# Modulation's rows one step ahead, latents' units early, compression units one by one, in a two-block kernel on one core

## The chip, the cores and the metric

The kernel runs on one core of one Trainium2 chip. The metric is the device time of one execution in microseconds (us). A core has five engines that run their own queues in order and meet at semaphores: TensorE (PE, matrix products into eight PSUM banks of 128 x 512 floats), VectorE (DVE), ScalarE (ACT), GpSimd (POOL) and SyncE (SP, which here only issues transfers). Behind SP's issues 16 DMA engines move the data from HBM.

## The reference, cut to what matters

Two transformer blocks over one sequence of 256 tokens, width 1024, in float32. What the change touches is the front of the first block:

```python
mod = (silu(c) @ w_ada + b_ada)                      # 6 x 1024: shift, scale, gate for attention and FFN
h = rms_norm(x, attn_norm) * (1.0 + scale_a) + shift_a
(nq, nkc, nvc, nks, nvs, nkw, nvw, ngate, cq, ckv, kr, bgate) = split(h @ w_in)
q_a = rope(rms_norm(heads(nq, 8), nsa_q_norm), pos)
kc = rms_norm(compress(rope(heads(nkc, 2), pos), cmp_k_pe, cmp_k_w1, cmp_k_w2), nsa_kc_norm)
vc = compress(heads(nvc, 2), cmp_v_pe, cmp_v_w1, cmp_v_w2)      # silu(blocks @ w1) @ w2
ks, kw = rope(rms_norm(nks)), rope(rms_norm(nkw))
q_b = rms_norm(cq, mla_cq_norm) @ w_uq               # latent cq: 384 wide
kv_b = rms_norm(ckv, mla_ckv_norm) @ w_ukv           # latent ckv: 256 wide; kr: rope part of the keys
```

Behind it come sparse and latent attention, the output projection, a gated FFN with a short convolution, and the second block; the change leaves their code as it is. All weights together are some 200 MB, each read once.

## The kernel before, in words

**Units.** Every weight matrix is cut into units of at most 1 MB. `_order()` (L62) writes down by hand in which order they are loaded; SP loads unit i into raw buffer i mod 5 (`sp_program`, L2451) and first waits until unit i-5 is used up (`freed`, L2438). SP's queue is in order, so a late buffer holds back every load behind it. A product is made of three float32r products of high and low parts: ACT copies the raw unit to a high part in two halves (`split_hi`, L330), DVE subtracts for the low part (`split_lo`, L340), PE multiplies (L386, L404). There are two buffers of each, so the high part of a unit waits until PE is done with the unit two before. `next_hi` and `next_lo` convert the unit behind the named one. Three kinds of units (ada, ck1, cv1) are used raw.

**Modulation.** Units ada 0 to 7 give scale and shift of the attention norm in four rounds. In round j PE multiplies ada 4+j and ada j into one row bank (`ada_rows_pe`, L504), ACT copies the bank to `rows[j % 2]` (L521), PE turns four pieces of it into columns of the same bank (`ada_turn_pe`, L528), DVE adds the bias and multiplies the two chunks 2j and 2j+1 of x with gain and rstd (`tail_dve`, L657), ACT and DVE split them into `H` (`tail_act`, L637). The rows of round j+1 wait until DVE has read the columns. Later units ada 8 to 10 are summed on DVE (`ada_dve`, L541), added over partitions by PE into a bank of ring G (`ada_sums_pe`, L563) and read by `mod_dve`.

**First projections.** wa (kc, vc, q0, q1: 48 matmuls) and wb (q2, q3: 24 matmuls) are cut along the contraction: pair j needs only chunks 2j and 2j+1 of `H`. `head_pe` (L620) runs statistics of x, rows 0, turn 0 and then, for each j: wa j, rows j+1, turn j+1, wb j.

**Banks.** PSUM banks 0 to 2 are ring G, 3 to 6 ring M (`Ring.take(reader)`, L127: the next bank in turn, and who must have read it before). Bank 7 holds the norm's statistics and the compression networks' sums. SBUF rings of four squares (`four_ring`), two rstd buffers and four temporaries work in the same way; a taker waits for the reader of its predecessor in the buffer.

**The other projections.** `proj_pe` (L872) and its ACT and DVE twins run win 0 (ks), 1 (kw), 4, 5, 6 (cq, ckv, kr), between them the rope and norm products of kc, q0 to q3 (`head_pe2`, L712), and behind each of win 4, 5, 6 two units of a compression network (`cmp2_pe`, 16 matmuls a unit, L772). `latent_pe` (L956) then runs win 2 and 3 (values), cv 2 and 3, the networks' second layers (`hidden_*`, `key_*`, `value_*`), the latents' statistics in bank 7 (`stat_pe`), ada 8, the gate rows wg, the rope of kr, uq 0 to 2, ada 9, ukv 0 and 1 with the MLA norms (`mla_stat_pe`), ada 10. The MLA tables are made on POOL (`latent_pool`, L1199) once the value product is copied.

Of the kernel before, what the change touches and what calls it, by code (L numbers as in the profile page):

```python
# [144 lines left out]
def build(nc, ins, out):  # L145
# [496 lines left out]
    def head_act(act):  # L642
# [8 lines left out]
        for j in range(4):  # L651
            ada_rows_act(act, j)
            tail_act(act, j)
            split_hi(act, ("wa", j))
            split_hi(act, ("wb", j))
# [2034 lines left out]
```

## Time and profile before

| | us |
|---|---|
| median of 3 runs (lowest, highest) | 1211.31 (1210.5, 1212.99) |
| the profiled execution's own time | 1205.75 |
| its span, first to last instruction | 1204.4 |
| PE busy in the span | 1134.9 (94%) |
| DVE busy | 749.7 (62%) |
| ACT busy | 591.0 (49%) |
| mean granted clock of TensorE | 0.972 |

The profiled execution is a run of its own, with its own time; sums over its rows stand against 1205.75, not against the median. Granted clock 1.00 is 2.4 GHz, 0.50 is 1.2 GHz. Times in rows are us from the start of the span; L386 is line 386 of the kernel. A row that begins with an engine and ends with an arrow names who ended the wait.

### The profile page before, as it was taken

What the parts mean: (1) busy time and instruction counts of PE and PEld (TensorE: products, weight loads), DVE (VectorE), ACT (ScalarE), POOL (GpSimd) and SP (SyncE); (2) the same over time, 40 slices, a digit from 0 to 9 for tenths busy, and PEclk for the clock granted to TensorE, in tenths of its full rate; (3) what the DMA queues carried; (4) which work ended last, traced back from release to release, by engine and by line L of the source; (5) the groups of instructions that cost most, each with busy time, mean ns of one, the idle gap of its engine ahead of it and who ended that gap; (6) DMA issues with size and microseconds to landing.
All of it is one profiled execution on the core that took longest, in us unless ns stands there. A gap on an engine that the chain in (4) does not pass through costs nothing.

```text
span 1204.4 us, 19238 instructions
## 1 busy us (share of the span) xinstructions
PE 1134.9 (94%) x7774; PEld 1027.3 (85%) x7774; DVE 749.7 (62%) x1411; ACT 591.0 (49%) x1046; POOL 27.8 (2%) x32
## 2 busy tenths in 40 slices
PE   5899789999999999999999899999999989999998
PEld 4797479888878999888988689999878968999986
DVE  2454567688757878866556666665455556666644
ACT  3362547345547566534434565445456357544533
POOL 0050100000000000001000000000000000000000
PEclk8999889889989999999989899999999999999999
DMA  8776362344334555465543265554544414655450
GB/s 323 300 288 248 122 236 106 105 175 175 141 105 158 175 180 189 143 259 211 190 143 105 70 234 206 175 181 175 176 168 158 140 42 138 223 177 185 147 192 35
DMA packets 30797, 207.81 MB, mean 173 GB/s; under 512 B 3540, under 2 KB 4052, under 8 KB 7157
## 3 DMA queue, kind: packets, MB, share of 16 engines
q1 hardware_dynamic: 30708, 206.58, 48.3%
q8 instruction: 62, 1.02, 0.3%
q14 instruction: 27, 0.21, 0.1%
HBM read 205.52 MB, written 1.05 MB: 172 GB/s over the span
## 4 chain that ended last, share of the span: by engine, by line
PE 84%; DVE 8%; ACT 5%; issue 2%; DMA 1%; SPq 0%; ACTq 0%; DVEq 0%
PE ps L386 47%; PE ps L1563 18%; PE ps L614 2%; DVE wlo L345 2%; PE ps L404 2%; ACT whi L338 1%; PE ps L2164 1%; PE ps L2196 1%; DVE tm L557 1%; PE ps L1262 1%; DMA raw<-win 1%; PE ps L1688 1%; PE ps L1340 1%; PE ps L516 1%; PE ps L772 1%
## 5 line engine op out<-in xcount | busy, mean ns | idle before, releaser
L345 DVE TENSOR_TENSOR wlo<-raw,whi 128x1024 fp32r<-128x1024 f32 (+2 forms) x328 | 370.9, 1174 | 246.1 <-ACT whi L338 246.0
L386 PE MATMUL ps<-H_h,whi 128*128 128x256 f32 x1552 | 447.0, 288 | 2.5 <-DVE wlo L345 2.5
L386 PE MATMUL ps<-H_l,whi 128*128 128x256 f32 x1552 | 440.9, 284 | 0.0
L386 PE MATMUL ps<-H_h,wlo 128*128 128x256 f32 x1552 | 440.8, 284 | 0.0
L338 ACT ACTIVATE whi<-raw 128x1024 fp32r<-128x1024 f32 (+2 forms) x328 | 314.8, 1010 | 183.6 <-PE ps L1563 112.9
L386 PEld LDWEIGHTS ps<-H_h,whi 128*128 128x128 f32 x1552 | 300.1, 193 | 6.9 <-issue 6.6
L386 PEld LDWEIGHTS ps<-H_l,whi 128*128 128x128 f32 x1552 | 299.9, 193 | 0.7 <-issue 0.5
L386 PEld LDWEIGHTS ps<-H_h,wlo 128*128 128x128 f32 x1552 | 299.5, 193 | 0.0
L1563 PE MATMUL ps<-whi,gl_h 128*128 128x512 f32 x264 | 105.6, 400 | 0.5 <-DVE wlo L345 0.5
L1563 PE MATMUL ps<-whi,gl_l 128*128 128x512 f32 x264 | 104.7, 396 | 0.0
L1563 PE MATMUL ps<-wlo,gl_h 128*128 128x512 f32 x264 | 104.6, 396 | 0.0
L1786 ACT ACTIVATE uw<-uw 128x256 f32<-128x256 f32 x66 | 27.4, 415 | 86.5 <-DVE uw L1877 86.4
L1563 PEld LDWEIGHTS ps<-whi,gl_h 128*128 128x128 f32 x264 | 49.7, 188 | 13.4 <-DVE wlo L345 1.4
L1563 PEld LDWEIGHTS ps<-wlo,gl_h 128*128 128x128 f32 x264 | 49.7, 188 | 12.1
L1563 PEld LDWEIGHTS ps<-whi,gl_l 128*128 128x128 f32 x264 | 49.7, 188 | 11.6
L1825 DVE SCALAR_TENSOR_TENSOR uw<-ps,par_sb,uw 128x255 f32<-128x255 f32 (+1 forms) x88 | 36.4, 476 | 25.2 <-ACT uw L1774 25.2
L1774 ACT ACTIVATE uw<-ps,par_sb 128x256 f32<-128x256 f32 x44 | 22.5, 562 | 46.5 <-PE ps L386 46.5
L557 DVE SCALAR_TENSOR_TENSOR tm<-raw,cs,tm 128x256 f32<-128x256 f32 x96 | 40.7, 479 | 0.0
L614 PE MATMUL ps<-H_h,whi 128*128 128x256 f32 x96 | 28.5, 297 | 8.3 <-DVE wlo L345 8.3
L1877 DVE TENSOR_TENSOR uw<-ps,rn 128x512 f32<-128x512 f32 x44 | 30.1, 684 | 2.3 <-PE ps L386 2.0
L1796 ACT ACTIVATE gl_h<-tm 128x256 fp32r<-128x256 f32 x66 | 27.5, 417 | 2.7 <-DVE tm L1792 2.7
L1563 PE MATMUL ps<-whi,H_h 128*128 128x512 f32 x64 | 26.2, 410 | 2.3 <-DVE wlo L345 2.0
(440 smaller groups left out, 1526.4 us busy)
## 6 DMA issues: line engine op xcount, KB each, us to landing
raw<-f SPq DMA_DIRECT2D x44, 1024.0 KB, 4.9
raw<-win SPq DMA_DIRECT2D x27, 1024.0 KB, 5.7
raw<-ada SPq DMA_DIRECT2D x24, 1024.0 KB, 5.9
raw<-up SPq DMA_DIRECT2D x22, 1024.0 KB, 4.9
raw<-g SPq DMA_DIRECT2D x20, 1024.0 KB, 4.8
raw<-pw SPq DMA_DIRECT2D x12, 1024.0 KB, 4.9
raw<-down SPq DMA_DIRECT2D x10, 1024.0 KB, 5.1
raw<-wa SPq DMA_DIRECT2D x4, 1024.0 KB, 7.5
```

Of the source, the lines that this page charges most:

```text
L338: act.activation(whi[j % NS][:, a:b], raw_of(key)[:, a:b], ACT.Copy).then_inc(w_hi.hit(key, half), 1)
L345: dve.tensor_tensor(wlo[j % NS][:, a:b], raw_of(key)[:, a:b], whi[j % NS][:, a:b].bitcast(F32), ALU.subtract).then_inc(w_lo.hit(key, half), 1)
L386: ins_ = pe.matmul(bank[:, m * 256:(m + 1) * 256], wt[a][:, kt * w + col + m * 128:kt * w + col + m * 128 + 128], act[b][:, k0 + kt, :], s ...
L404: ins_ = pe.matmul(bank[:, t * width:(t + 1) * width], act[b][:, kt, t * 128:(t + 1) * 128], wt[a][:, kt * w + col:kt * w + col + width], ...
L557: dve.scalar_tensor_tensor(out=o, in0=w, scalar=cs[:, kt:kt + 1], in1=o, op0=ALU.mult, op1=ALU.add).then_inc(ada_sum.hit(u, kt), 1)
L614: ins_ = pe.matmul(where["win", name][:, m * 256:(m + 1) * 256], wt[a][:, c:c + 128], H[b][:, k, :], start=k == 0 and m == 0 and i == 0, s ...
L1563: ins_ = pe.matmul(b[t][:], act[h][:, k0 + kt, t * 128:(t + 1) * 128], wt[a][:, kt * 512:(kt + 1) * 512], start=k0 + kt == 0 and i == 0 an ...
L1774: act.activation(w[:, m, :], z[:, m, :], ACT.Identity, bias=pc("b_conv", 2 * c + m), scale=pc("w_conv", (2 * c + m) * 3 + 2)).then_inc(u_i ...
L1786: act.activation(w[:, g, :], w[:, g, :], ACT.Silu).then_inc(u_silu.hit(n, c), 1)
L1796: act.activation(gl[0][:, c, :], where["tm", n, c][:, 0:256], ACT.Copy).then_inc(g_hi.hit(n, c), 1)
L1825: dve.scalar_tensor_tensor(out=w[:, m, s:], in0=z[:, m, 0:256 - s], scalar=pc("w_conv", (2 * c + m) * 3 + 2 - s), in1=w[:, m, s:], op0=ALU ...
L1877: dve.tensor_tensor(uw[c % 3][:], v2(where[n, c][:]), bc2(rn[:]), ALU.mult).then_inc(u_rn.hit(n, c), 1)
```

## The change

- Load order: the ada units come earlier against wa and wb; win 4, 5, 6 come before win 1, 2, 3; ck1 and cv1 units are spread one behind each win or uq unit; wg before ada 8.
- Rows: `ada_rows_pe(j)` waits for ACT's copy of row j-1 (`ada_row`) instead of DVE's reading; the turned columns go to bank 7, columns 256 + 4j. PE's order in the head is written out, as are ACT's and DVE's. 14 matmuls of ones with ones are put ahead of the statistics.
- `proj_*`: order win 0, 4, 5, 6, 1, 2, 3; the latents' squares are taken with the copy into their own buffers (`ckq`, two of them the modulation's row buffers), their statistics go to ring M (`latent_stat_pe`), their norms are done here; ck 0 to 3 and cv 0 one unit behind each. ACT's conversion of the unit after next ahead of the ks copy goes.
- `latent_*`: wg, rope of kr, key product, cv 1, uq 0, key norm, ada 8, cv 2, uq 1, cv 3, uq 2, hidden layer of v, ada 9, ukv 0 with the value product in its middle. POOL's MLA tables no longer wait for the value copy.
- Four buffers move: `xb` to the place of `X`, `hid` behind `ckvn`, `krb` to `rn`, `sqkr` into a row buffer; x^T is therefore loaded before ada 11, when cv 3 is done.

The diff below leaves out the ACT and DVE twins where they follow PE's order, and code that moves as a block.

```diff
@@ -66,11 +66,14 @@
     def seq(name, a=0, b=None):
         out.extend((name, i) for i in range(a, len(UNITS[name]) if b is None else b))
 
-    for i in range(4):
-        seq("ada", 4 + i, 5 + i), seq("ada", i, i + 1), seq("wa", i, i + 1), seq("wb", i, i + 1)
-    seq("win", 0, 2), seq("win", 4, 5), seq("ck1", 0, 2), seq("win", 5, 6), seq("ck1", 2, 4), seq("win", 6, 7)
-    seq("cv1", 0, 2), seq("win", 2, 3), seq("cv1", 2, 4), seq("win", 3, 4), seq("ada", 8, 9)
-    seq("wg"), seq("uq", 0, 2), seq("ada", 9, 10), seq("uq", 2), seq("ukv", 0, 1), seq("ada", 10, 11), seq("ukv", 1)
+    seq("ada", 4, 5), seq("ada", 0, 1), seq("wa", 0, 1), seq("ada", 5, 6), seq("ada", 1, 2), seq("wb", 0, 1)
+    seq("wa", 1, 2), seq("ada", 6, 7), seq("ada", 2, 3), seq("ada", 7, 8), seq("ada", 3, 4), seq("wb", 1, 2)
+    for i in (2, 3):
+        seq("wa", i, i + 1), seq("wb", i, i + 1)
+    seq("win", 0, 1), seq("win", 4, 6), seq("ck1", 0, 1), seq("win", 6, 7), seq("ck1", 1, 2), seq("win", 1, 2)
+    seq("ck1", 2, 3), seq("win", 2, 3), seq("ck1", 3, 4), seq("win", 3, 4), seq("cv1", 0, 1), seq("wg"), seq("ada", 8, 9)
+    seq("cv1", 1, 2), seq("uq", 0, 1), seq("cv1", 2, 3), seq("uq", 1, 2), seq("cv1", 3, 4), seq("ada", 9, 10), seq("uq", 2)
+    seq("ukv", 0, 1), seq("ada", 10, 11), seq("ukv", 1)
     seq("win", 7, 10), seq("ada", 11, 13), seq("win", 10, 11), seq("ada", 13, 14), seq("win", 11, 12)
     seq("ada", 14, 16), seq("win", 12, 13), seq("ada", 16, 17), seq("win", 13, 14), seq("ada", 17, 19)
     seq("win", 14, 15), seq("ada", 19, 20), seq("wo")
...
+    ckq = [sb("ckq", [128, 512]), rows[1], rows[0]]
     xc = [sb(f"xc{i}", [128, 2, 256]) for i in range(2)]
     hrow = [sb(f"hrow{i}", [128, 256]) for i in range(2)]
+    cw2 = [sb(f"cw2{i}", [128, 256]) for i in range(2)]
+    place[0] = X_at
     xb = [sb(f"xb{i}", [128, 32, 32]) for i in range(2)]
     place[0] = attn
     grow = sb("grow", [24, 256])
...
@@ -509,7 +515,7 @@
             if u == 4:
                 pe.wait_ge(*c_silu(2))
             elif c0 == 0:
-                pe.wait_ge(*mod_set(j - 1))
+                pe.wait_ge(*ada_row(j - 1))
             r = raw_of(("ada", u))
             for kt in range(8):
                 g = 32 * (kt % 4)
@@ -525,13 +531,15 @@
             act.wait_ge(*ada_col(j - 2))
         act.activation(rows[j % 2][:], where["rows"][:], ACT.Copy).then_inc(ada_row.hit(j), 1)
 
+    def mod_cols(j):
+        return banks[7][:, 256 + 4 * j:260 + 4 * j]
+
     def ada_turn_pe(pe, j):
 
-        b = where["rows"]
         pe.wait_ge(*ada_row(j))
         pe.wait_ge(*const_set("pick"))
         for m in range(4):
-            ins_ = pe.matmul(b[:, m:m + 1], rows[j % 2][:, m * 128:m * 128 + 128], pick[:, 0:1], start=True, stop=True)
+            ins_ = pe.matmul(mod_cols(j)[:, m:m + 1], rows[j % 2][:, m * 128:m * 128 + 128], pick[:, 0:1], start=True, stop=True)
         ins_.then_inc(ada_col.hit(j), 1)
 
     def asum(u):
...
@@ -619,19 +627,28 @@
 
     def head_pe(pe):
         pe.wait_ge(*const_set("ones"))
-        where["rows"], _ = M.take(mod_set(3))
+        where["rows"], _ = M.take(ada_row(3))
         for name in FIRST:
             ring = G if name in FIRST[0:3] else M
             where["win", name], _ = ring.take(z_copy(name) if name in ("kc", "vc") else z_sq(name))
+        for _ in range(14):
+            pe.matmul(where["rows"][:, 0:128], ones[:], ones[:], start=True, stop=True)
         for p in range(4):
             stat_pe(pe, "x0", p, where["sq", "x0", p], 2, p == 0, p == 3, sq_set("x0", p))
         ada_rows_pe(pe, 0)
         ada_turn_pe(pe, 0)
-        for j in range(4):
+        first_pe(pe, "wa", 0)
+        ada_rows_pe(pe, 1)
+        first_pe(pe, "wb", 0)
+        ada_turn_pe(pe, 1)
+        ada_rows_pe(pe, 2)
+        first_pe(pe, "wa", 1)
+        ada_turn_pe(pe, 2)
+        ada_rows_pe(pe, 3)
+        first_pe(pe, "wb", 1)
+        ada_turn_pe(pe, 3)
+        for j in (2, 3):
             first_pe(pe, "wa", j)
-            if j < 3:
-                ada_rows_pe(pe, j + 1)
-                ada_turn_pe(pe, j + 1)
             first_pe(pe, "wb", j)
...
+    def latent_stat_pe(pe, n, k0, m):
+
+        sm, old = M.take(rs_ln(n))
+        if old:
+            pe.wait_ge(*old)
+        where["sm", n] = sm
+        for k in range(k0, k0 + m):
+            pe.wait_ge(*sq_set("ck", k // 2))
+            ins_ = pe.matmul(sm[:, 0:256], ones[:], ckq[k // 2][:, k % 2 * 256:k % 2 * 256 + 256], start=k == k0,
+                             stop=k == k0 + m - 1)
+        ins_.then_inc(ones_done.hit(n), 1)
...
     def proj_pe(pe):
         gemm_pe(pe, ("win", 0), H, held, z_sq("ks"))
         pe.wait_ge(*con_in())
         head_pe2(pe, "kc")
+        gemm_pe(pe, ("win", 4), H, held, sq_set("ck", 0))
+        head_pe2(pe, "q0")
+        gemm_pe(pe, ("win", 5), H, held, sq_set("ck", 1))
+        head_pe2(pe, "q1")
+        cmp_pe(pe, "ck", 0)
+        gemm_pe(pe, ("win", 6), H, held, sq_set("ck", 2))
+        latent_stat_pe(pe, "vs", 0, 3)
+        head_pe2(pe, "q2")
+        cmp_pe(pe, "ck", 1)
         gemm_pe(pe, ("win", 1), H, held, z_sq("kw"))
-        head_pe2(pe, "q0")
-        for i in range(3):
-            gemm_pe(pe, ("win", 4 + i), H, held, ev_act("ck", i))
-            head_pe2(pe, ("q1", "q2", "q3")[i])
-            if i == 2:
-                hidden_pe(pe, 0)
-            cmp2_pe(pe, *(("ck", 0), ("ck", 2), ("cv", 0))[i])
+        latent_stat_pe(pe, "vw", 3, 2)
+        head_pe2(pe, "q3")
+        cmp_pe(pe, "ck", 2)
+        values_pe(pe, "vs", ("win", 2))
+        head_pe2(pe, "ks")
+        cmp_pe(pe, "ck", 3)
+        values_pe(pe, "vw", ("win", 3))
+        head_pe2(pe, "kw")
+        hidden_pe(pe, 0)
+        cmp_pe(pe, "cv", 0)
...
         next_hi(act, ("win", 0))
         first("q2")
         first("q3")
-        next_hi(act, ("win", 1))
         head_copy_act(act, "ks", where["win", 0], unit("win", 0))
         next_hi(act, ("win", 4))
+        latent_copy_act(act, 0)
         head_act2(act, "q0")
+        next_hi(act, ("win", 5))
+        latent_copy_act(act, 1)
+        head_act2(act, "q1")
+        next_hi(act, ("win", 6))
+        latent_copy_act(act, 2)
+        latent_rstd_act(act, "vs", 3)
+        for k in range(3):
+            norm_hi(act, "vs", k, cqn)
+        head_act2(act, "q2")
+        next_hi(act, ("win", 1))
         head_copy_act(act, "kw", where["win", 1], unit("win", 1))
...
@@ -982,6 +1068,8 @@
             pe.wait_ge(*old)
         where["pm", "kr"] = pm
         pe.matmul(pm[:, 0:256], cc("perm32"), CK[:, 5, :], start=True, stop=True).then_inc(perm_done.hit("kr"), 1)
+        key_pe(pe)
+        cmp_pe(pe, "cv", 1)
         for i in range(3):
             for half in range(2):
                 b, old = G.take(ev_act("uq", i, half))
@@ -998,6 +1086,11 @@
                 pe.wait_ge(*gt_set(1))
                 pe.transpose(b[:, 0:24], grow[:, 0:128], cc("ident")[0:24, 0:24])
                 pe.transpose(b[:, 24:48], grow[:, 128:256], cc("ident")[0:24, 0:24]).then_inc(gt_turn.hit(), 1)
+                key_norm_pe(pe)
+                ada_sums_pe(pe, 8)
+            if i < 2:
+                cmp_pe(pe, "cv", 2 + i)
+        hidden_pe(pe, 1)
         ada_sums_pe(pe, 9)
         for half in range(4):
             b, old = G.take(ev_act("ukv", 0, half))
@@ -1006,6 +1099,8 @@
             where["ukv", 0, half] = b
             mm_fm(pe, ("ukv", 0), ckvn, normed("vw") if half == 0 else held, b, half * 256,
                   done=unit.hit("ukv", 0) if half == 3 else half_done.hit("ukv", 0, half))
+            if half == 1:
+                value_pe(pe)
             pm, old = M.take(rope_b("mq", half))
...
@@ -1089,6 +1168,7 @@
                 dst = mq[:, c0:c0 + 2, :] if i < 2 else mqr[:, c0 - 8:c0 - 6, :]
                 act.activation(dst, v2(where["uq", i, half][:]), ACT.Copy).then_inc(ev_act.hit("uq", i, half), 1)
         next_hi(act, ("ukv", 0))
+        hidden_act(act, 1)
         for half in range(4):
...
@@ -1145,14 +1207,20 @@
             next_lo(dve, ("uq", i))
             if i == 0:
                 ada_dve(dve, 9)
+            if i == 1:
+                key_norm_dve(dve)
+                mod_dve(dve, 8)
         dve.wait_ge(*gt_turn())
         dve.tensor_copy(gt[:], where["gt"][:, 0:48].rearrange("p (t g) -> p t g", g=24)).then_inc(gt_set.hit(2), 1)
         mod_dve(dve, 9)
         next_lo(dve, ("ukv", 0))
+        hidden_dve(dve, 1)
         for half in range(4):
             mq_rope_dve(dve, half)
             if half:
                 mq_norm_dve(dve, half - 1)
+            if half == 2:
+                value_dve(dve)
         next_lo(dve, ("ukv", 1))
         ada_dve(dve, 10)
         for half in range(4):
@@ -1197,7 +1265,6 @@
             m_rope.hit("mk", p), 1)
 
     def latent_pool(pool):
-        pool.wait_ge(*cmp_set("v"))
         table_pool(pool, "mq", "mq_rope", "mq_rsw", "cosr", "sinr")
...
                 sp.dma_start(con[:], ins["con"]).then_inc(con_in.hit(), 16)
-            if key == ("win", 4):
+            if key == ("ck1", 0):
                 load_bc(sp, 0)
-                sp.wait_ge(*n_lo("A", 7))
+            if key == ("win", 1):
                 for k, n in enumerate(("ck2", "cv2")):
                     sp.dma_start(cw2[k][:], ins[n].rearrange("(p f) -> p f", p=128)).then_inc(cw2_in.hit(k), 16)
             if key in BC_AT:
                 n, last = BC_AT[key]
                 sp.wait_ge(*mt_mul(last, 1, 1))
                 load_bc(sp, n)
-            if key == ("win", 6):
+            if key == ("ada", 11):
+                sp.wait_ge(*unit("cv1", 3))
                 sp.dma_start(X[:].rearrange("p t d -> p (t d)"), ins["xt"]).then_inc(xt_in.hit(), 16)
```

## Rows read from the trace of the kernel before

**Rows 1.** The page, part 1: busy us (share) and instructions of each engine.

```profile
PE 1134.9 (94%) x7774; PEld 1027.3 (85%) x7774; DVE 749.7 (62%) x1411; ACT 591.0 (49%) x1046; POOL 27.8 (2%) x32
```

**Rows 2.** Stretches: us; busy us of PE, PEld, DVE, ACT, POOL; clock, DMA share, GB/s.

```profile
20.40:72.70 52.30, 46.07 (x410) 42.07 (x411) 21.48 (x39) 18.08 (x29) 9.76 (x10) 0.97 0.79 299
72.70:175.40 102.70, 88.50 (x664) 73.27 (x663) 57.34 (x91) 44.19 (x79) 12.01 (x12) 0.92 0.55 204
175.40:205.00 29.60, 28.81 (x179) 26.44 (x177) 23.11 (x46) 23.88 (x41) 0.00 (x0) 1.00 0.35 139
```

**Rows 3.** Stretches, short ones, same columns.

```profile
0.00:10.00 10.00, 2.74 (x7) 2.24 (x8) 1.00 (x12) 3.68 (x6) 0.20 (x4) 1.00 0.83 317
20.30:23.70 3.40, 3.24 (x15) 3.24 (x16) 2.44 (x4) 0.84 (x2) 0.00 (x0) 0.50 0.70 266
126.20:133.00 6.80, 6.00 (x39) 2.61 (x38) 4.33 (x9) 1.70 (x4) 0.00 (x0) 0.50 0.11 28
...
154.80:160.30 5.50, 5.50 (x22) 5.13 (x23) 0.42 (x1) 0.00 (x0) 0.00 (x0) 0.50 0.85 311
```

**Rows 4.** PE's waits, 12.3 to 72.7 us: sum, times, longest.

```profile
PE ps L614 <- DVE wlo L345: 8.3, 4, 4.4
PE ps L534 <- ACT arow L526: 3.1, 4, 0.8
```

**Rows 5.** The chain of waits in time, 26 to 43 us: start, us, what.

```profile
27.90 1.91 PE ps L516 x32
...
30.54 1.07 PE ps L534 x8
```

**Rows 6.** PE's waits, 72.7 to 175.4 us.

```profile
PE ps L573 <- DVE tm L557: 8.1, 1, 8.1
...
PE ps L726 <- DVE tm L738: 2.1, 1, 2.1
PE ps L788 <- DVE tm L738: 1.1, 1, 1.1
```

**Rows 7.** Timeline of PE, the start: start, us, instruction, count, idle before.

```profile
7.26 3.35 PE L455 MATMUL ps<-sq,ones 128*128 128x256 f32 x8 [7.26 <-ACT sq L447]
10.45 1.89 PE L455 MATMUL ps<-zt,ones 128*128 128x256 f32 x8
```

**Rows 8.** DMA issues of 95.2 to 97 us: count, KB each, median us to landing.

```profile
raw<-cv SPq DMA_DIRECT2D x2, 1024.0 KB, 7.5
raw<-win SPq DMA_DIRECT2D x1, 1024.0 KB, 4.7
```

**Rows 9.** Timelines of ACT, DVE and POOL between 79 and 93 us.

```profile
86.78 0.60 ACT L710 ACTIVATE sq<-ps 128x512 f32<-128x512 f32 x1 [5.77 <-PE ps L726]
...
79.61 2.36 DVE L345 TENSOR_TENSOR wlo<-raw,whi 128x1024 fp32r<-128x1024 f32 x2 [2.44 <-ACT whi L338]
...
88.36 3.12 DVE L345 TENSOR_TENSOR wlo<-raw,whi 128x1024 fp32r<-128x1024 f32 x2 [4.46 <-ACT whi L338]
...
83.98 6.42 POOL L936 TENSOR_TENSOR xb<-xc,par_sb 128x240 f32<-128x240 f32 x8 [14.30 <-DVE xc L741]
```

**Rows 10.** The chain of waits in time, between 84 and 147 us.

```profile
86.75 5.74 PE ps L386 x48
...
94.21 1.86 PE ps L772 x32
...
145.73 0.99 PE ps L851 x8
```

**Rows 11.** Timeline of DVE, 164 to 170 us.

```profile
164.75 1.82 DVE L345 TENSOR_TENSOR wlo<-raw,whi 128x1024 fp32r<-128x1024 f32 x2
166.49 0.61 DVE L554 TENSOR_SCALAR tm<-raw,cs 128x256 f32<-128x256 f32 x2
167.01 2.46 DVE L557 SCALAR_TENSOR_TENSOR tm<-raw,cs,tm 128x256 f32<-128x256 f32 x6
```

**Rows 12.** The chain of waits in time, 175 to 179 us.

```profile
175.85 1.80 ACT whi L338 x2
```

More of the change, by code:

```diff
@@ L209, in build @@
     ckvn = pair("ckvn", 2)
+    hid = [sb(f"hid{i}", [128, 2, 30]) for i in range(4)]
     place[0] = mv_at
@@ L650, in head_act @@
         rstd(act, "x0", stat("x0", 3), D, banks[7][:, 0:256], rst[0])
[L651 to L655, printed above, removed]
+        ada_rows_act(act, 0)
+        tail_act(act, 0)
+        split_hi(act, ("wa", 0))
+        split_hi(act, ("wb", 0))
+        ada_rows_act(act, 1)
+        split_hi(act, ("wa", 1))
+        tail_act(act, 1)
+        ada_rows_act(act, 2)
+        split_hi(act, ("wb", 1))
+        tail_act(act, 2)
+        ada_rows_act(act, 3)
+        split_hi(act, ("wa", 2))
+        tail_act(act, 3)
+        for key in (("wb", 2), ("wa", 3), ("wb", 3)):
+            split_hi(act, key)
     def tail_dve(dve, j):
-        b = where["rows"]
+        b = mod_cols(j)
         dve.wait_ge(*ada_col(j))
@@ L866, in gemm_pe, with latent_rstd_act, latent_norm_dve, values_pe @@
         mm_fm(pe, key, act, ready, b, 0, by_k=by_k, done=unit.hit(*key), hook=hook)
-    def cmp2_pe(pe, nm, a):
-        cmp_pe(pe, nm, a)
-        cmp_pe(pe, nm, a + 1)
+    def latent_stat_pe(pe, n, k0, m):
[8 more added lines that the diff above has]
+        ins_.then_inc(ones_done.hit(n), 1)
+    def latent_rstd_act(act, n, m):
+        buf, old = rst_ring.take(n_mul(n, m - 1))
+        where["r", n] = buf
+        rstd(act, n, ones_done(n), 128 * m, where["sm", n][:, 0:256], buf, free=old)
+    def latent_norm_dve(dve, n, k0, m, lat, gain):
+        dve.wait_ge(*rs(n))
+        for k in range(m):
+            x = temp(dve, ("tm", n, k), n_lo(n, k))
+            dve.scalar_tensor_tensor(out=x[:, 0:256], in0=CK[:, k0 + k, :], scalar=pc(gain, k),
+                                     in1=where["r", n][:, 0:256], op0=ALU.mult, op1=ALU.mult).then_inc(n_mul.hit(n, k), 1)
+            if k:
+                norm_lo(dve, n, k - 1, lat)
+        norm_lo(dve, n, m - 1, lat)
+    def values_pe(pe, n, key):
+        b, old = G.take(ev_act(n))
+        if old:
+            pe.wait_ge(*old)
+        where[key] = b
+        mm_tm(pe, key, H, held, b, 0, 256, unit.hit(*key))
     def proj_pe(pe):
@@ L887, in latent_copy_act, with values_act @@
         act.activation(CK[:, 2 * i:2 * i + 2, :], v2(where["win", 4 + i][:]), ACT.Copy).then_inc(ev_act.hit("ck", i), 1)
+        act.activation(ckq[i][:], where["win", 4 + i][:], ACT.Square).then_inc(sq_set.hit("ck", i), 1)
+    def values_act(act, n, key, dst):
+        act.wait_ge(*unit(*key))
+        act.activation(dst[:], v2(where[key][:]), ACT.Copy).then_inc(ev_act.hit(n), 1)
     def proj_act(act):
@@ L916, in proj_dve @@
         next_lo(dve, ("win", 0))
-        next_lo(dve, ("win", 1))
         head_dve2(dve, "kc")
@@ L956, in latent_pe @@
     def latent_pe(pe):
-        for n, key, k0, m in (("vs", ("win", 2), 0, 3), ("vw", ("win", 3), 3, 2)):
-            b, old = G.take(ev_act(n))
-            if old:
-                pe.wait_ge(*old)
-            where[key] = b
-            mm_tm(pe, key, H, held, b, 0, 256, unit.hit(*key))
-            if n == "vs":
-                head_pe2(pe, "ks")
-                key_pe(pe)
-                cmp2_pe(pe, "cv", 2)
-                head_pe2(pe, "kw")
-            else:
-                hidden_pe(pe, 1)
-                key_norm_pe(pe)
-            for k in range(m):
-                stat_pe(pe, n, k, where["sq", n, k], 1, k == 0, k == m - 1, sq_set(n, k))
-        value_pe(pe)
-        ada_sums_pe(pe, 8)
         b, old = G.take(gt_exp())
@@ L1058, in latent_act @@
     def latent_act(act):
-        for n, key, dst, lat, k0, m in (("vs", ("win", 2), vs, cqn, 0, 3), ("vw", ("win", 3), vw, ckvn, 3, 2)):
-            if n == "vw":
-                next_hi(act, key)
-            act.wait_ge(*unit(*key))
-            act.activation(dst[:], v2(where[key][:]), ACT.Copy).then_inc(ev_act.hit(n), 1)
-            if n == "vs":
-                head_act2(act, "ks")
-                key_act(act)
-                cmp_row_act(act, 1)
-            else:
-                head_act2(act, "kw")
-                hidden_act(act, 1)
-                key_norm_act(act)
-            for k in range(m):
-                square(act, CK[:, k0 + k, :], n, k, ev_act("ck", (k0 + k) // 2), n=256, ring=four_ring)
-            buf, old = rst_ring.take(n_mul(n, m - 1))
-            where["r", n] = buf
-            rstd(act, n, stat(n, m - 1), 128 * m, banks[7][:, 0:256], buf, free=old)
-            for k in range(m):
-                norm_hi(act, n, k, lat)
-        sq_ring.free[:], zt_ring.free[:] = four_ring.free[0:2], four_ring.free[2:4]
         next_hi(act, ("wg", 0))
```

79 lines of the change are left out of this document (43 added, 36 removed).

## The prediction

> **What bounds the kernel now.** I read the page's engine totals first, then the stretches of the span, then the waits and the chain inside the stretches that the change touches. TensorE (PE) is busy for 94% of the span [rows 1], so only PE's own idle or slow time can be won. The table of stretches says where that is [rows 2]: from 20.4 to 72.7 us (the first projections) PE is busy 46.07 of 52.30 us, from 72.7 to 175.4 (the other projections, compression networks, latents) 88.50 of 102.70, from 175.4 to 205.0 28.81 of 29.60. The 999.4 us behind 205.0 run code that the change leaves as it is. At stake are 6.2 + 14.2 us idle, and what PE loses where its clock was granted at 0.50 (1.2 instead of 2.4 GHz), which is half of its busy time there: 3.24 / 2 = 1.6 us in the first stretch and (6.00 + 5.50) / 2 = 5.75 us in the second [rows 3].
>
> The first stretch's idle is 3 rounds of about 0.77 + 1.27 us: of the four waits of each kind in the view the first lies before it, at the start [rows 4]. PE computes a round of modulation rows (1.91), waits for ScalarE's copy, turns them (1.07) [rows 5], projects with the old half of the weights and waits for DVE's low part of the next. The second stretch's idle is one wait of 8.1 us before the sums of modulation unit 8 and four smaller ones, 2.1 and 1.1 among them, that make the other 6 [rows 6].
>
> The profiled execution took 1205.75 us, 1.35 more than its span. The median of the runs is 1211.31, 5.56 higher. I sum against the former and carry the difference over to the latter.
>
> **A, the start: -0.9 us.** 14 matmuls of ones are put before the statistics. PE idles there until the squares come at 7.26. Of the 8 statistic matmuls the first four take 3.35 us and the last four 1.89 [rows 7], so PE was at 1.2 GHz for the first four. Fourteen of half that width cost 14 x 0.42 = 5.9 us at 1.2 GHz (3.35 / 4 / 2 each), from 1.1 to 7.0: hidden, and PE comes warm to 7.26. The statistics then end at about 10.7 instead of 12.3. Modulation units 4 and 0 must have landed: 317 GB/s over the first 10 us [rows 3] is 3.17 of the 3.35 MB of parameters, x and both units, so they are there at about 10.5. All that follows is 1.65 earlier. The stretch at 1.2 GHz up to 23.7 stays, I assume; it held 15 matmuls in 3.24 us and now holds 23, and each of these 8 is worth 0.12 at the end: 0.9 is what arrives. Bounds: 0 (no warming) to -2.5 (the slow stretch goes too).
>
> **B, rows one step ahead: -5.9 us.** The rows of round j+1 wait only for the copy of round j, since the turned columns go to bank 7. wb(0) lies between rows 1 and their turn, so the copy lies under 2.9 us of matmuls. Round by round: rows 1 from 27.0, wb(0) from 28.9, turn 31.8, rows 2 from 32.9 to 34.8; wa(1) needs normalised chunk 2, made from the turn's end by DVE, ScalarE and DVE in 2.2 us: 35.1. That is the one wait, 0.3. Afterwards each low part is ready before its turn. SP's queue: modulation unit 2 is issued when PE has used unit 5 (28.0) and lands 4.7 us later [rows 8] at 32.7, 1 us before PE asks. 6.2 - 0.3 = 5.9. Bounds: -6.2, and -3 if each transfer lands as late as the 7.5 us of a queued one [rows 8]. The head ends at 72.7 - 6.8 = 65.9.
>
> **C, units behind units: -6.7 us.** The old losses go: 14.2 idle + 5.75 slow = 19.95. Two new waits come.
> First: ScalarE's queue has the square of ks before the high part of win 5. It overwrites the buffer that q0's ones-matmul reads and so waits for that matmul: 5.77 us in the old kernel [rows 9]. There PE had a whole unit (5.74) [rows 10] in between; now win 5 is the very next unit behind q0. Square 0.6, first high half 1.0, first low half 1.2, with their handovers 2.9 us: PE waits that. The POOL tables for MLA, moved up from behind the value sums to right behind the windows, lie beside this conversion. A low part beside POOL's windows took 3.12 for two halves, 2.36 alone [rows 9]; half of 0.76 is 0.4. Together 3.3. Bounds 2.5 to 4.5.
> The Trainium skill (SBUF — State Buffer, on the port pair of DVE and GpSimd) says that an operation of DVE with two SBUF inputs and a GpSimd operation that reads SBUF exclude each other for a whole instruction. The 3.12 beside the 2.36 agrees in kind; by the rule in full the first half could stand behind one whole POOL instruction, 0.8 by the windows' row (6.42 for 8), and the wait would be 3.7.
> Second, the large one: the sums of modulation 8 take the third G bank. Counting takes of that ring of three (win 0, 4, 5, 6, 1, 2, 3, gate weights, key, uq 0 twice), it is the bank of the key product, free once DVE has made the normalised key. On DVE that step stands behind the low part of uq 2, and this behind all the sums of modulation 9. Behind the waiting PE instruction are queued compression unit cv 2, all of uq 1 and of uq 2. The race runs from K, the end of kw's ones-matmul. DVE: rstd on ScalarE 1.35, last rope product 0.65, hidden layer 1.0, low part of uq 0 1.8, sums of modulation 8 0.6 + 2.5 [rows 11]: K + 7.9, which frees its raw buffer. Only then SP issues cv 3, modulation 9 and uq 2, in this order. The first of three lands after 4.7, the second 2.5 later [rows 8]: K + 15.1. Sums of 9 3.1, low part of uq 2 1.8 [rows 11], key 0.3: K + 20.3. PE: hidden layer 0.6, two compression units 2 x 0.93, gate rows 24 x 0.12 = 2.9, rope of kr 0.4, key 0.5, uq 0 36 x 0.12 = 4.3, turns 0.35 [rows 10]: K + 10.9. PE waits 9.4 us. In the old kernel PE was at 1.2 GHz for 5.5 us after its 8.1 us of waiting [rows 3, 6]; I take the same, a loss of 2.7. Together 12.0. Bounds 0 to 15.
> The work that leaves the stretch (value product 0.99 [rows 10], second hidden layer 0.63, sums of modulation 9 0.43) is 2.05. The stretch becomes 102.7 - 19.95 - 2.05 + 3.3 + 12.0 = 96.0.
>
> **D, the 29.6 us behind it: +1.2.** The value product, 0.99, now lies in a stretch that PE fills. The second hidden layer and the sums of 9 lie under ScalarE's conversion of ukv 1 (1.80) and the square behind it [rows 12], which stays; the exponential adds 0.2 to it. DVE's 1.0 for the hidden layer and 0.4 for the copy go into its idle time. Bounds 0.8 to 2.5.
>
> **At nothing:** x^T is loaded behind win 9 instead of beside win 6, where SP's queue is idle, and its reader comes some 100 us later. cw2's wait for the norm goes; nobody waited for it. kr's square is saved (0.4 of a ScalarE that waits anyway). Behind 205.0, E = 0, bounds -2 to +3 for slow stretches that fall otherwise.
>
> Sum: -0.9 - 5.9 - 6.7 + 1.2 = -12.3. Own time 1205.75 - 12.3 = 1193.45; as a median 1211.31 - 12.3 = 1199.0.
>
> **Rivals.**
> 1. The clock falls at the first new wait too: 3.3 us before win 5 send PE to 1.2 GHz, as from 126.2 on, behind waits of 2.1 and 1.1 [rows 3, 6]. A stretch of 6.8 us like that one, less what of it is idle, costs 3.0: -9.3, 1202.0. Against: two waits in each round before 63 us (0.8 and 1.3) did not cool it.
> 2. The ring wait isn't there or is hidden, since I count takes: 12.0 more is gained, 1187.0. Against: the count and the order on DVE are plain to read.
> 3. The reordering doesn't do what it says: each old wait of the second stretch is replaced by one of like length, because SP's chain of five buffers, each freed by the step before it, sets the pace. C = 0: -5.6, 1205.7. For: two new waits worth 15.3 against 19.95 are already in my sum. Against: in my walk the other transfers have 5 us to spare.
> 4. Slower: behind the long wait before modulation 8's sums PE stays at 1.2 GHz. Each us there costs 0.5, so 2 x (12.3 + 2.4) = 29 us more at 1.2 GHz, to about 185, make it +2.4: 1213.7. From there on it decides. For: the wait is longer than the old one. Against: after 8.1 us of waiting PE was back within 5.5 us [rows 3].
>
> **Chances.** Forecast 0.52 (own range 1195 to 1203), rival 1 0.17, rival 2 0.12, rival 3 0.11, rival 4 0.05, no change 0.03. The range of 1190 to 1206 holds the forecast, rival 1, rival 3 and the side of rival 2 on which only a part of the wait goes; what it leaves out is the rest of rival 2, rival 4 and no change. A measurement of this kernel can't tell less than 0.2% (2.4 us) from no change. Faster is all but rival 4 and no change: 0.92, same 0.03, slower 0.05.
>
> **What would show it.** A: 8 statistic matmuls in about 3.5 us. B: PE's waits for ScalarE's copy gone, the head's last matmul near 65.9. C: ScalarE's square of ks waiting some 8 us, and PE then some 3 for DVE's low part; PE idle some 9 us before modulation 8's sums with DVE's key step as releaser, at about 137 to 147. D: last matmul before the attention near 192.7. Wrong: no idle before those sums (rival 2), a head that ends behind 69, or PE at 1.2 GHz for more than 20 of the first 200 us.

## The result, and the profile after

The changed kernel takes 1194.69 us (median of 4 runs, 1193.6 to 1199.0) beside 1211.07 for the kernel before; the ratio is 0.9869, 95% interval 0.9842 to 0.9896. That is 16.4 us less, where 12.3 were forecast (1199.0, range 1190 to 1206). Five further rounds (e1) gave 1197.05 beside 1211.28, ratio 0.9894 (0.9862 to 0.9926). The forecast's own narrower range, 1195 to 1203, is missed by 0.3 in the first and holds the second. The two first profiled executions are only 6.75 apart (1199.0 and 1205.75), and the forecast for the changed kernel's own, 1193.45, is missed by 5.6; why is told below.

The page of the changed kernel, part 1, and its stretches (columns as in [rows 2]; the ends lie where the head, uq 2 and ukv 1 end, the answers to [rows 2]):

```profile
PE 1139.8 (95%) x7802; PEld 1033.5 (86%) x7802; DVE 748.5 (62%) x1411; ACT 590.9 (49%) x1043; POOL 25.9 (2%) x32
```

```profile
20.40:64.90 44.50, 44.02 (x404) 41.04 (x404) 20.15 (x37) 18.04 (x29) 9.31 (x10) 0.96 0.85 340
64.90:165.90 101.00, 86.41 (x655) 71.73 (x653) 55.13 (x87) 43.86 (x75) 10.61 (x12) 0.92 0.50 186
165.90:196.80 30.90, 30.45 (x190) 27.62 (x189) 24.18 (x50) 24.00 (x42) 0.00 (x0) 1.00 0.53 214
81.90:85.30 3.40, 3.33 (x15) 3.36 (x16) 3.33 (x5) 3.37 (x6) 1.76 (x1) 0.50 0.31 82
...
150.80:157.00 6.20, 6.17 (x31) 4.08 (x31) 0.42 (x1) 0.00 (x0) 0.00 (x0) 0.50 0.13 36
```

The head ends at 64.9 instead of 72.7, its idle of 6.2 us [rows 2] is 0.5. The middle stretch is 101.0 long instead of 102.7: 14.6 us idle, and two slow stretches, 81.9 to 85.3 and (0.50 from 143.4 on) 150.8 to 157.0. PE's waits up to 230 us, answering [rows 4, 6] (sum, times, longest; the 4.4 is the start, as before, and 3.9 is the attention's):

```profile
PE ps L581 <- DVE kcn L874: 11.6, 1, 11.6
PE ps L622 <- DVE wlo L351: 4.4, 1, 4.4
PE ps L1379 <- DVE sq L1363: 3.9, 2, 2.4
PE ps L392 <- DVE wlo L351: 3.0, 1, 3.0
...
PE ps L542 <- ACT arow L532: 0.8, 1, 0.8
PE ps L622 <- DVE H_l L505: 0.5, 1, 0.5
```

Both new waits of the forecast are there by name. The first, on the timelines of ACT, DVE and POOL (answering [rows 9]): the square of ks sits 7.72 us for q0's ones-matmul, the conversion of win 5 behind it starts at 79.51, its low part at 80.59.

```profile
79.02 0.60 ACT L744 ACTIVATE sq<-ps 128x512 f32<-128x512 f32 x1 [7.72 <-PE ps L760]
79.51 1.99 ACT L344 ACTIVATE whi<-raw 128x1024 fp32r<-128x1024 f32 x2
```

```profile
80.59 2.36 DVE L351 TENSOR_TENSOR wlo<-raw,whi 128x1024 fp32r<-128x1024 f32 x2 [7.62 <-ACT whi L344]
82.87 0.88 DVE L770 TENSOR_TENSOR tm<-q,tab_qc 128x512 f32<-128x512 f32 x1
```

```profile
80.23 0.94 POOL L1031 TENSOR_SCALAR tab_mkc<-con_sb,par_sb 128x256 f32<-128x256 f32 x1
81.13 2.53 POOL L1032 TENSOR_SCALAR tab_mks<-con_sb,par_sb 128x256 f32<-128x256 f32 x1
```

The second, on DVE's timeline: modulation 8's sums, gate and rope, the low part of uq 1, then 5.06 us for the transfer of modulation 9, its sums, the low part of uq 2, and last the key (kcn) for which PE stands still.

```profile
133.24 2.46 DVE L565 SCALAR_TENSOR_TENSOR tm<-raw,cs,tm 128x256 f32<-128x256 f32 x6
...
138.98 1.83 DVE L351 TENSOR_TENSOR wlo<-raw,whi 128x1024 fp32r<-128x1024 f32 x2 [0.25 <-ACT whi L344]
145.86 0.62 DVE L562 TENSOR_SCALAR tm<-raw,cs 128x256 f32<-128x256 f32 x2 [5.06 <-DMA raw<-ada]
146.40 2.46 DVE L565 SCALAR_TENSOR_TENSOR tm<-raw,cs,tm 128x256 f32<-128x256 f32 x6
148.79 1.83 DVE L351 TENSOR_TENSOR wlo<-raw,whi 128x1024 fp32r<-128x1024 f32 x2
150.53 0.24 DVE L874 SCALAR_TENSOR_TENSOR kcn<-ps,par_sb,rst 128x30 f32<-128x30 f32 x1
```

### The profile page after: what moved, and what is told of

It reads as the page before. It is cut to its first block, busy times and chain, and to the rows that moved or that the text cites. A ratio compares the mean times of both kernels' runs of the same rounds, so it can differ in the third digit from the quotient of the medians.

```text
span 1197.7 us, 19285 instructions
## 1 busy us (share of the span) xinstructions
PE 1139.8 (95%) x7802; PEld 1033.5 (86%) x7802; DVE 748.5 (62%) x1411; ACT 590.9 (49%) x1043; POOL 25.9 (2%) x32
## 4 chain that ended last, share of the span: by engine, by line
PE 84%; DVE 8%; ACT 4%; issue 2%; DMA 1%; SPq 0%; ACTq 0%; DVEq 0%
PE ps L392 47%; PE ps L1630 18%; PE ps L622 3%; PE ps L410 2%; DVE wlo L351 2%; DVE tm L565 1%; ACT whi L344 1%; PE ps L2231 1%; PE ps L2263 1%; DMA raw<-ada 1%; PE ps L1329 1%; PE ps L1755 1%; PE ps L581 1%; PE ps L1131 1%; PE ps L1407 1%
## 5 line engine op out<-in xcount | busy, mean ns | idle before, releaser
L392 PE MATMUL ps<-H_l,whi 128*128 128x256 f32 x1552 | 442.5, 285 | 0.0
L392 PEld LDWEIGHTS ps<-H_h,whi 128*128 128x128 f32 x1552 | 301.4, 194 | 10.4 <-issue 10.2
L1630 PEld LDWEIGHTS ps<-whi,gl_l 128*128 128x128 f32 x264 | 49.7, 188 | 11.6
L622 PE MATMUL ps<-H_l,whi 128*128 128x256 f32 x96 | 28.2, 294 | 0.0
```

What stands on the lines that cost most here:

```text
L392: ins_ = pe.matmul(bank[:, m * 256:(m + 1) * 256], wt[a][:, kt * w + col + m * 128:kt * w + col + m * 128 + 128], act[b][:, k0 + kt, :], s ...
L622: ins_ = pe.matmul(where["win", name][:, m * 256:(m + 1) * 256], wt[a][:, c:c + 128], H[b][:, k, :], start=k == 0 and m == 0 and i == 0, s ...
L1630: ins_ = pe.matmul(b[t][:], act[h][:, k0 + kt, t * 128:(t + 1) * 128], wt[a][:, kt * 512:(kt + 1) * 512], start=k0 + kt == 0 and i == 0 an ...
```

## The experiments

Each ratio is to the kernel before, run in the same group. e1 to e4 are one group, e5 to e8 and e9 to e12 the others; the kernel before took 1211.28, 1210.70 and 1212.21 in them. Where e5 to e12 are set against e1 in us, two groups are compared, so the profiles are the surer ground. The table cuts every profiled span in three: the head (first statistic matmul to the end of the first projections), the middle (from there to the first matmul of the attention) and what lies behind, whose code the change leaves as it is. All are us, taken from the chains of waits.

| profile | head | middle | behind |
|---|---|---|---|
| before, first | 65.4 | 132.3 | 999.4 |
| before, e10 and e11 | 66.4 and 66.0 | 132.6 and 132.5 | 1003.8 and 1003.7 |
| changed, first | 57.7 | 131.9 | 1000.9 |
| changed, e1 | 58.3 | 129.7 | 1000.9 |
| e2, head alone | 57.7 | 133.1 | 1003.9 |
| e3, rest alone | 67.6 | 129.7 | 999.5 |
| e4, key earlier | 58.5 | 121.1 | 1002.6 |
| e5, conversion first | 57.7 | 125.1 | 1001.1 |
| e6, both | 58.4 | 115.8 | 1001.1 |
| e7, without the 14 matmuls | 59.6 | 130.4 | 998.5 |
| e8, ukv 1 first | 58.3 | 115.7 | 1001.0 |
| e9, pairs | 57.6 | 115.1 | 1000.8 |
| e12, old row wait | 59.0 | 129.5 | 1002.7 |

Behind the attention's first matmul the code is the same, and still the profiles differ by 5.4 us there. A total alone therefore can't say what a step in the head or the middle is worth.

**The changed kernel again (e1).** No edit.

> The changed kernel once more, beside the kernel before on the same chip. The timed runs so far say -16.4 us, the two profiled executions -6.75. Theory: the gain in typical executions is what the runs say, and one profiled execution of each can be off by 5 us because the slow stretches of TensorE's clock and the landing of transfers fall otherwise: median 0.985 to 0.989 of the kernel before, and a new profile with a span near 1193. Rival: the true gain is that of the profiled pair, and the runs were on different chips: about 0.994.

Measured 1197.05 us, ratio 0.9894 (0.9862 to 0.9926). The theory holds in the main, though 0.9894 is a little above its range of 0.985 to 0.989; the rival's 0.994 is outside the interval. The span of its profile, 1195.7, is above the 1193 named. PE waits 9.9 us at the ring instead of 11.6, because modulation 9 landed sooner.

**The head alone (e2).** The kernel before with the hunks of the diff for `_order` (first lines), `ada_rows_pe`, `mod_cols`, `head_*` and `tail_*`, nothing else.

> The kernel before with the head of the change alone: load order of ada, wa and wb, rows one step ahead, columns in bank 7, the 14 matmuls of ones; the projections, latents and buffers stay as they were. Theory (steps A and B): -6.8 predicted, -7.8 by the changed kernel's trace (its head ends at 64.9 instead of 72.7): 1203 to 1204.5, ratio about 0.9936. Rival: the second part waits for transfers or clock, so that an earlier head is given back there: less than -3, ratio above 0.9975.

Measured 1202.54, ratio 0.9924 (0.9897 to 0.9951), 8.7 less than the 1211.28 beside it. The head brings more than half of the gain. In the profiles it ends at 64.81 instead of 73.25 (e10), 8.4 sooner, and of that 0.5 is given back in the middle (133.1 against 132.6) and nothing behind. The old 8.1 us wait stands as it stood.

```profile
PE ps L577 <- DVE tm L561: 8.1, 1, 8.1
PE ps L618 <- DVE wlo L347: 4.4, 1, 4.4
PE ps L756 <- DVE tm L768: 2.2, 1, 2.2
```

**The rest alone (e3).** The changed kernel with the same hunks undone.

> The changed kernel with the old head (old load order of ada, wa and wb, old row waits, columns in the row bank, no matmuls of ones); the rest as changed. Theory by the profiled pair: from the head's end to the last matmul before attention 132.3 us before and 131.9 after, so nearly nothing: -0.5, ratio about 0.9995. Rival by steps C and D of the prediction: -5.5, 0.9955; by the runs' total less the head, -8.6: 0.993. The wait for DVE's low part behind q0 (3.0 us) and the wait before the sums of modulation 8 (some 10 us) are both there.

Measured 1205.02, ratio 0.9957 (0.994 to 0.9975), 6.3 less. So C and D are real; the profiled pair's ratio of 0.9995 is outside the interval. But the prediction's -5.5 is met by the total only: the middle, where C and D lie, is 129.7 instead of 132.6 in the profiles, -2.9; the rest of the total lies outside it. -8.7 and -6.3 add to -15.0; the whole was -14.2 beside the same runs of the kernel before. Both new waits are there:

```profile
PE ps L580 <- DVE kcn L847: 9.3, 1, 9.3
PE ps L390 <- DVE wlo L349: 3.0, 1, 3.0
```

The middle and what lies behind in this profile (columns as in [rows 2]):

```profile
74.60:204.20 129.60, 116.13 (x840) 98.64 (x839) 79.31 (x137) 68.01 (x116) 10.61 (x12) 0.95 0.51 195
204.20:1203.70 999.50, 963.67 (x6473) 879.74 (x6471) 643.67 (x1217) 496.20 (x887) 5.79 (x6) 0.98 0.45 160
```

**The key's norm earlier on DVE (e4).**

```diff
             if i == 0:
+                key_norm_dve(dve)
                 ada_dve(dve, 9)
             if i == 1:
-                key_norm_dve(dve)
                 mod_dve(dve, 8)
```

> The changed kernel with one step moved on VectorE: the key's norm product before the sums of modulation 9 instead of behind the low part of uq 2. Theory: this product frees the third bank of ring G, so the wait of 11.6 us before the sums of modulation 8 goes; TensorE runs cv 2 and uq 1 at once and then waits for uq 2's low part, which still stands behind modulation 9 and its landing. uq 2 would start at about 151 at the earliest (its low half's start by the trace) instead of 161.3, and the clock falls less: -8 to -11 against the changed kernel, ratio to the kernel before about 0.979. Rival: the transfer of modulation 9 and the conversion behind it set the pace, TensorE only waits later: less than -4.

Measured 1189.47, ratio 0.9824 (0.9791 to 0.9858), 7.6 less than e1. The wait of 9.9 us is now 1.5 and PE isn't slow behind it. This shows that the wait was the ring's bank and no lack of data: modulation 9 lands only 0.9 us sooner (its sums start at 143.26, in e1 at 144.13), and PE never waits for it or for uq 2, whose matmuls follow cv 3 at 148.7. The middle is 8.6 us shorter (121.1 against 129.7), 8 to 11 being expected, although 2.1 us come back in it as a longer wait for the square behind ukv 1's conversion, 2.6 instead of 0.5. The expectation was for the total, and 7.6 falls just short of it. In the profile what lies behind took 1.7 more: at 188.6 the clock is at 0.50 for 6.8 us, where e1 has 3.4 (at 198.6).

```profile
PE ps L392 <- DVE wlo L351: 3.0, 1, 3.0
PE ps L1131 <- ACT sq L1140: 2.6, 1, 2.6
PE ps L581 <- DVE kcn L874: 1.5, 1, 1.5
```

**ScalarE's conversion ahead of the square (e5).**

```diff
-        head_copy_act(act, "ks", where["win", 0], unit("win", 0))
         next_hi(act, ("win", 4))
+        head_copy_act(act, "ks", where["win", 0], unit("win", 0))
```

> The changed kernel with two steps of ScalarE swapped: the high part of win 5 before the copy and square of ks. Theory: the wait of 3.0 us for VectorE's low part behind q0 goes, because the high part no longer stands behind a square that waits for q0's ones-matmul, and with it the slow clock from 81.9 to 85.3 us (1.7 more). Everything behind moves up 4.5 us; the later wait before the sums of modulation 8 has its chain started by kw's ones-matmul and moves with it. About -4.5 against the changed kernel, some 1191.5. Rival: the transfers behind it (their buffers are freed by DVE's conversions) or the later wait swallow it: less than -1.5.

Measured 1191.2, ratio 0.984 (0.9815 to 0.9864), 5.9 less than e1. The middle is 4.6 us shorter (125.1 against 129.7), as expected. The 3.0 is gone from the waits, and from 76 to 90 us PE is busy throughout at a granted clock of 1.00. The 9.9 stands: the first is independent of the second.

**Both (e6).** The edits of e4 and e5.

> The changed kernel with both mends: the high part of win 5 before the square of ks, and the key's norm product before the sums of modulation 9. If the two waits are independent, the gains add: -4.5 and -7.6 against the changed kernel (the second as measured: 1189.5 beside 1197.05), about 1185. Rival: the second mend leaves a chain of transfers (uq 2, ukv 1) that an earlier start only makes TensorE wait for: nearer to 1188.

Measured 1184.74, ratio 0.9793 (0.977 to 0.9816), 12.3 less than e1 where 7.6 + 5.9 = 13.5 would be the sum. They add, within the scatter; in the middle it is 13.9 (115.8 against 129.7) where 8.6 + 4.6 = 13.2 would be the sum.

**Without the 14 matmuls (e7).** The loop of `head_pe` left out.

> The changed kernel without the 14 matmuls of ones. Theory (step A): they bring 0.9 us net; without them the 8 statistic matmuls take 5.1 us again instead of 3.46 and the first rows start 1.6 later, of which the slow stretch of the clock behind gives half back: +0.9, between +0 and +1.7. Rival: they also decide how long the clock is slow up to 24 us; then +2.5 or more, or a gain from leaving them out.

Measured 1198.74, ratio 0.9907 (0.9886 to 0.9927), 1.7 more than e1; the intervals overlap. The trace is sharper. The head, from the first statistic matmul to its end, is 67.42 - 7.80 = 59.6 us, in e1 65.15 - 6.84 = 58.3: 1.3 less. The eight profiles that have the 14 matmuls and the new row wait lie between 57.6 and 58.5, so they bring 1.2 to 2.0. Up to the first rows it is 5.8 instead of 3.7 us, 2.1 more where 1.6 were expected; the head behind gives 0.8 of it back.

**ukv 1 before modulation 10 (e8).** The edits of e6 and

```diff
-    seq("ukv", 0, 1), seq("ada", 10, 11), seq("ukv", 1)
+    seq("ukv", 0, 1), seq("ukv", 1), seq("ada", 10, 11)
```

> Both mends of e6, and ukv 1 loaded before modulation 10, so that its raw buffer is the one that uq 1's conversion frees and not the one of cv 3. In e4 TensorE waited 2.6 us for a square behind ukv 1's high part, whose transfer was issued only when cv 3 was done (148.7) and landed at 155.5. Theory: that wait falls to the 0.5 of the changed kernel: -2 against e6, about 1183. Rival: ScalarE's own order (copies of uq 2 before the conversion) holds it as long: no difference.

Measured 1183.27, ratio 0.9773 (0.975 to 0.9796): the lowest median here, 1.5 less than e6 with intervals that overlap. The mechanism that I named is not it: PE's wait for that square is 0.5 in e6 already, and 0.5 here. The middle is 115.7 instead of 115.8, so no gain of this edit is shown.

**Units of the compression network in pairs (e9).** On e8, with PE's units moved to match (ck 0 and 1 behind q2, ck 2 and 3 behind ks), the load order:

```diff
-    seq("win", 0, 1), seq("win", 4, 6), seq("ck1", 0, 1), seq("win", 6, 7), seq("ck1", 1, 2), seq("win", 1, 2)
-    seq("ck1", 2, 3), seq("win", 2, 3), seq("ck1", 3, 4), seq("win", 3, 4), seq("cv1", 0, 1), ...
+    seq("win", 0, 1), seq("win", 4, 7), seq("ck1", 0, 2), seq("win", 1, 3)
+    seq("ck1", 2, 4), seq("win", 3, 4), seq("cv1", 0, 1), ...
```

> The kernel of e8 with the key network's units in pairs again: load order win 4, 5, 6, ck1 0, 1, win 1, 2, ck1 2, 3, win 3; TensorE runs ck 0 and 1 behind q2 and ck 2 and 3 behind ks. Theory: one unit behind each unit of weights is no gain of its own once win 4, 5, 6 come first; all loads of this stretch still land before ScalarE asks: 1183 to 1184, as e8. Rival: pairs free two raw buffers late and at once, and the next weights land late, as win 6, 2 and 3 did in the kernel before (18.4 us of ScalarE waiting): 1187 or more.

Measured 1183.59, ratio 0.9769 (0.9752 to 0.9787), the same as e8. One unit behind each unit is no gain by itself there; the middle is even 0.6 us shorter in pairs (115.1 against 115.7). This was tried for the key network alone and with both waits mended. That the gain of the middle comes with the latents' units first is what remains, but no run has that order without the rest.

**The kernel before, two more profiles (e10, e11).** No edit.

> The kernel before, for a second profile. The first one took 1205.75 us at a mean granted clock of 0.972; most executions of this kernel take about 1211 at 0.967. Theory: the difference of 5 us is slow clock alone (0.005 x 1204 / 0.5 = 12 us more at 1.2 GHz, half of which is lost), in stretches behind 205 us that the change doesn't touch, as e2's profile has them at 573 and 973 us. Rival: slow transfers or longer waits in the first 205 us.

> The same again, since one execution in three or four is of the 0.972 kind: theory and rival as for the other profile of the kernel before.

Measured 1210.95 and 1210.33 at a mean clock of 0.967 both, so the two answer alike. Up to 205 us they repeat the first profile within 0.9 us: the first matmul of the attention begins at 205.85 and 205.33, in the first profile at 205.01. Behind it e10 needs 1003.8 us, the first profile 999.4. These slow stretches of e10 have no counterpart in the first profile:

```profile
581.00:584.40 3.40, 2.81 (x13) 2.85 (x14) 2.37 (x5) 0.00 (x0) 0.00 (x0) 0.51 0.31 55
980.40:987.20 6.80, 6.80 (x22) 4.67 (x21) 3.32 (x9) 4.83 (x10) 0.00 (x0) 0.50 0.00 0
```

with a third, at 618.6, of 10.2 us where the first profile has 6.8. In the 36 timed runs of the kernel before that the three groups hold, 7 have a mean clock of 0.972 or more and take 1202.3 to 1207.24; 29 have 0.967 and take 1210.07 to 1213.76. The first profile was of the rarer kind. Theory held.

**The old wait of the rows in the new order (e12).** `ada_rows_pe` waits for `mod_set(j - 1)` again.

> The changed kernel with the old wait of the rows: rows j+1 wait until VectorE has read the turned columns of round j; PE's order, bank 7 and the load order stay as changed. Theory: rows 1 come after reading 0 long since, rows 2 and 3 come right behind turns 1 and 2 and wait for VectorE's reading, some 0.3 us each: +0.6 at most, the head ends at 65.5. So it is the order (wb between rows and turn) that brings step B. Rival: the wait itself was the matter: +3 or more.

Measured 1198.7, ratio 0.9878 (0.9853 to 0.9903), no difference from e1 that can be told. From the first statistic matmul to the head's end it is 66.95 - 7.92 = 59.0 us, 0.7 more than e1; PE waits for the reading twice, 1.3 in sum, where the expectation had 0.6. So the wait, and with it the bank of its own for the columns, is worth some 0.7 (0.6 to 1.5 beside the eight profiles named at e7). The rest of step B stands without it: it comes with the new order, with wb between the rows and their turn. That order came together with the new load order of ada, wa and wb; how much of it PE's order would bring with the old loads was not tried.

## Why the prediction was right, and where its sizes were not

The order of events and the sum came out; the sizes of two terms did not, and they partly cancelled. The forecast was summed against the first profile of the kernel before. In the first pair of profiles the parts are -7.8 for the head (64.9 against 72.7, forecast -6.8), -0.4 for the middle (131.9 against 132.3, forecast -5.5) and +1.5 behind (forecast 0), together the -6.7 between the spans. So by the sum's own yardstick C missed by far. That profile of the kernel before was of the rarer, faster kind, and the changed kernel's first had the longest ring wait, 11.6. The comparison that is fair in kind is e1's profile against e10's, 1195.7 and 1209.7, 13.9 apart:

```profile
65.20:194.90 129.70, 116.26 (x841) 98.78 (x839) 79.30 (x137) 67.89 (x116) 10.60 (x12) 0.95 0.52 196
194.90:1195.70 1000.80, 964.67 (x6471) 879.88 (x6470) 643.95 (x1217) 496.20 (x887) 5.79 (x6) 0.98 0.45 159
```

```profile
73.30:205.90 132.60, 117.27 (x841) 99.93 (x839) 80.40 (x137) 68.02 (x119) 11.98 (x12) 0.94 0.50 189
205.90:1209.60 1003.70, 969.00 (x6471) 883.65 (x6470) 643.78 (x1217) 496.46 (x887) 5.79 (x6) 0.97 0.45 159
```

**A and B, forecast -6.8, measured -8.1** (65.2 against 73.3). The order of events is as forecast, with the small wait for H_l (0.5, forecast 0.3) included. The statistics take 3.46 us in the changed kernel's first profile (forecast 3.4). In e1 they take 3.72. The difference between -6.8 and -8.1 is mostly the old side: the head took 66.4 in e10 and 65.4 in the first profile, and 0.66 of that is the statistics (5.74 and 5.08). e7 parts the two steps: A is 1.3 (59.6 to 58.3, forecast 0.9), B 6.8 against e10 (66.4 to 59.6) and 5.8 against the first profile, forecast 5.9. That the first statistic matmuls ran at half speed is read from their durations; the profile's clock stands at 1.00 there [rows 3]. e7 bears the reading out: without the matmuls of ones the first eight records take 3.75 us and the next eight 2.29, with them 1.99 and 1.89 (e1).

**C and D, forecast -5.5, measured -2.9 in this pair and -6.3 in the runs of e3.** The runs include what the clock does behind, so -2.9, which e3's own profile has too, is the part that can be laid beside my terms: forecast 126.8 us (96.0 + 30.8), measured 129.7. D is right (30.9 in the first profile after, forecast 30.8); C is the term that was mis-sized. The wait behind q0 was 3.0 (3.3, the POOL surcharge of 0.4 did not come). The ring wait was 9.9 and 11.6 (9.4): the release is DVE's key step as named, and K + 20.3 would be 148.5 against 149.4 in e1 (kw's ones-matmul ended at 128.2). The loads behind modulation 8 were issued at K + 7.8 (7.9), and modulation 9 landed 7.8 us later (7.2 in my walk), in the first profile 9.7: that is its longer wait. The slow time behind it ran from 149.4 to 154.3 in e1, a loss of 2.5 (2.7). Two terms were missing. The clock also fell at the first wait, which was rival 1 and cost 1.7, less than its 3.0: win 5 took 7.47 instead of 5.76. And a compression unit alone costs more than half a pair, see below: about 1.1 together, an estimate from 0.26 for each of four more changes between narrow and wide matmuls. 3.0 + 9.9 + 2.5 + 1.7 + 1.1 = 18.2 of new losses against 15.3.

**E, forecast 0 with bounds of -2 and +3, measured -2.9** (1000.8 against 1003.7). PE is busy for 969.00 us with the old and 964.67 with the new kernel on the same instructions, so this is the clock, and idle time grew by 1.4. It lies outside its bounds in this pair and inside them in the first (+1.5), and it made up for what C missed. Nothing in the change aims at it, and the profiles, none of which has other code there, lie between 998.5 and 1003.9. Six of the ten with the changed middle have 1000.8 to 1001.1, so the change may bring this along; how is not shown. That the total came out close (13.9 or 14.2 against 12.3) is partly this cancelling, which is luck.

Rival 2 (no ring wait) and rival 3 (C worth nothing) fell by the waits of the changed kernel and by e3, rival 4 by PE being back at full speed at 157.0 (154.3 in e1). One of the prediction's signs of being wrong came true all the same: the clock was at 0.50 for 23.9 of the first 200 us (21.9 in e1), and more than 20 was named. The sign was badly set, since the kernel before has 23.9 too; PE was busy in 14.8 of them before and in 14.6 after. Rival 2 is what one moved line makes of the kernel: e4.

The Trainium skill (SBUF — State Buffer, "SBUF: two separate sides") says that a DVE operation with two SBUF inputs and a POOL operation that reads SBUF exclude each other for a whole instruction, whichever starts first. It was weighed with 3.7 us for the first wait if DVE's low part stood behind a POOL instruction. Measured was 3.0. The low part began at 80.59, inside a table's 80.23 to 81.17, and took 2.36 all the same, as if alone; by the rule it should have waited for that table, so here the trace differs (POOL's spans are rough). The table that began at 81.13 took 2.53 instead of 0.94, as if it had waited for the low part to end at 82.95, and there the trace agrees. DVE's rope product behind it took 0.88 instead of 0.68. In this case it was mostly the table instruction that paid.

## What to carry to other kernels

Before moving steps, count the takes of each ring and ask where on its own queue the reader of the predecessor now stands: a reader of 0.24 us that slid behind a transfer and two conversions cost 10 us, and one line moved gave 7.6 back. A conversion queued behind a step that waits for a buffer wants to go first (e5). And take a second profile of the old kernel before summing against it: its first one was 5 us off the typical run. When several steps are worth a few us each, compare the stretch that a step touches, not the totals: 5.4 us of scatter lay behind it here.
